# Half of one projection's columns multiplied inside the attention that runs before it

## The reference, cut to what matters

```python
proj = jnp.einsum('bsd,de->bse', rmsnorm(x, norm_w), w_in)
aq, ak, av, ag, bq, bk, bv, bg, iq, ik, iw = jnp.split(proj, split_at, axis=-1)
# group A: differential attention, 4 heads, two score maps each
p = softmax(q1 k1 * scale + bias) - lam * softmax(q2 k2 * scale + bias)
ao = rmsnorm(p v, subln_w) * (1 - lambda_init) * silu(ag)
# group B: 8 heads, each query sees only its 256 best keys by an indexer score
score = sum_h iw_h * relu(iq_h . ik);  sel = top_k(score, 256)
bo = softmax(q k[sel] * scale + bias) v[sel] * silu(bg)
y = x + concat(ao, bo) @ w_out;  return rmsnorm(y, final_norm_w)
```

## Time and profile before

| | us |
|---|---|
| median of 3 runs (lowest, highest) | 804.96 (803.58, 806.73) |
| the profiled execution: its time, its span | 805.53, 803.7 |
| first attention (PE's first score product to its last v product) | about 252.4 to 377 |
| projections of group B on PE | 377.5 to 551.8 |
| second half of the selection and the mask on DVE | 382.9 to 547.9 |
| second attention | 551.8 to about 700 |

### The profile page before, as it was taken

One profiled execution on the slowest core, in us unless ns is written; L12 is line 12 of the kernel. 1 busy time (PEld: TensorE's weight loads), 2 busy tenths in 40 slices (PEclk: granted clock), 3 DMA queues, 4 the chain that ended last, 5 costly groups with the idle time before them and its releaser, 6 DMA issues.

```text
span 803.7 us, 11774 instructions
## 1 busy us (share of the span) xinstructions
PE 759.5 (94%) x4161; PEld 634.3 (79%) x4161; DVE 630.1 (78%) x1347; ACT 305.3 (38%) x677; POOL 318.6 (40%) x383
## 2 busy tenths in 40 slices
PE   4899999999999888899999999999999999999996
PEld 3665888888887877788888888887888888888885
DVE  3738999999999988986999999996667676534343
ACT  5437222131315665677131220305545554422121
POOL 5220122124637775813255443647997600300000
PEclk9999999999999999999999999999999999999999
DMA  7142111111110101030211212110303100121231
GB/s 275 53 120 65 40 51 42 53 53 40 53 40 1 27 2 27 8 112 18 63 47 45 53 53 53 40 52 28 84 24 106 27 2 1 35 99 65 103 106 52
DMA packets 21489, 44.55 MB, mean 55 GB/s; under 512 B 3076, under 2 KB 5816, under 8 KB 21304
## 3 DMA queue, kind: packets, MB, share of 16 engines
q1 hardware_dynamic: 21432, 43.81, 18.5%
HBM read 35.40 MB, written 6.57 MB: 52 GB/s over the span
## 4 chain that ended last, share of the span: by engine, by line
PE 86%; DVE 7%; ACT 3%; issue 2%; DMA 1%; SPq 0%; POOL 0%; DVEq 0%; ACTq 0%
PE psum L990 43%; PE psum L1095 11%; PE psum L1153 11%; PE psum L1077 5%; PE psum L1052 4%; PE psum L1055 3%; PE psum L929 3%; PE psum L957 2%; DVE small L1331 2%; DVE probs L1385 1%; ACT probsT_B L804 1%; DVE small L1376 1%; DMA xs<-in_x 1%; PE psum L878 1%; PE psum L1063 1%
## 5 line engine op out<-in xcount | busy, mean ns | idle before, releaser
L511 POOL TENSOR_TENSOR w_lo<-w_raw,w_hi 128x512 fp32r<-128x512 f32 x64 | 83.1, 1300 | 244.4 <-ACT w_hi L660 244.0
L1312 DVE MATCH_REPLACE8 score<-top,score 128x384 f32<-128x384 f32 (+2 forms) x192 | 165.8, 876 | 0.0
L1307 DVE MAX8 top<-score 128x8 f32<-128x384 f32 (+2 forms) x192 | 155.5, 879 | 1.1
L660 ACT ACTIVATE w_hi<-w_raw 128x512 fp32r<-128x512 f32 x64 | 40.3, 630 | 240.4 <-PE psum L990 240.4
L990 PE MATMUL psum<-big_hi,w_hi 128*128 128x512 f32 x256 | 99.8, 390 | 0.3 <-POOL w_lo L511 0.3
L990 PE MATMUL psum<-big_hi,w_lo 128*128 128x512 f32 x256 | 99.6, 389 | 0.0
L990 PE MATMUL psum<-big_lo,w_hi 128*128 128x512 f32 x256 | 99.6, 389 | 0.0
L990 PE MATMUL psum<-w_hi,big_hi 128*128 128x512 f32 x256 | 99.6, 389 | 0.0
L990 PE MATMUL psum<-w_lo,big_hi 128*128 128x512 f32 x256 | 99.6, 389 | 0.0
L990 PE MATMUL psum<-w_hi,big_lo 128*128 128x512 f32 x256 | 99.6, 389 | 0.0
L793 ACT ACTIVATE probs<-psum,small 128x384 f32<-128x384 f32 (+7 forms) x112 | 83.0, 742 | 30.7 <-DVE small L1352 16.3
(11 more groups left out here) (156 smaller groups left out, 1505.4 us busy)
## 6 DMA issues: line engine op xcount, KB each, us to landing
w_raw<-in_w_in SPq DMA_DIRECT2D x64, 256.0 KB, 2.6
xs<-in_x SPq DMA_DIRECT2D x8, 512.0 KB, 6.5
k_high_twice<-k_high_twice SPq DMA_DIRECT2D x16, 256.0 KB, 3.7
xres<-in_x SPq DMA_DIRECT2D x8, 512.0 KB, 3.7
out_y<-y_out SPq DMA_DIRECT2D x16, 256.0 KB, 2.1
w_tail<-in_w_out SPq DMA_DIRECT2D x10, 256.0 KB, 2.6
bias_scratch<-bias_row SPq DMA_DIRECT2D x1, 2304.0 KB
bias<-bias_scratch SPq DMA_DIRECT2D x12, 128.0 KB, 3.1
```

The costliest lines, as they stand in the source:

```text
L511: pool.tensor_tensor(w_lo[:, r, 0:cols], w_raw[:, r, 0:cols], w_hi[:, r, 0:cols].bitcast(f32), ALU.subtract).then_inc(w_lo_made, 1)
L660: act.activation(w_hi[:, n % SW, 0:cols], w_raw[:, n % SW, 0:cols], ACT.Copy).then_inc(w_hi_made, 1)
L1307: ins = dve.max(top8[:, i - SEL0, :], sc)
L1312: ins = dve.match_replace(sc, top8[:, i - SEL0, :], sc, TAKEN)
```

## The change

The columns of group B's query projection (chunks 40 to 47) are cut differently: a chunk now is half of the 1024 rows (4 row blocks) of 128 columns. The first four chunks, `FILLS` = 40 to 43, which give column blocks 0 and 1 of the queries (four output banks), are multiplied inside the first attention: in iterations 1 to 32 PE does `fill`, three products of 512 columns, between the transposes of step s-1 and the map 1 scores. They gather in bank 4 (`FILL_BANK`), so the scores keep banks 0 to 3. Every 8th iteration ends a bank, and ACT moves it out (`move_fill`). After the attention PE does only the other half (`project_rest`), 96 products where there were 192, and goes on with the three other groups.

Chunks 40 to 43 get their own places: raw in slot 0 of `w_raw` and in a new `wf_raw`, the parts in `wf_hi` and `wf_lo`, which lie on what were a fourth `probs` buffer and `probs_x`. So `probs` has two buffers for map 0 and one for map 1.

```diff
+        Q_GROUP = B_GROUPS[0]
+        Q0 = Q_GROUP * DB
+        FILLS = range(Q0, Q0 + 4)
+        FILL_BANK = 4
...
-            if m == 0:
-                return probs[:, s % 3, :]
-            return probs[:, 3, :] if s % 2 == 0 else probs_x[:, 0, :]
+            return probs[:, s % 2 if m == 0 else 2, :]
-        S_BANKS, O_BANK, T_BANK = 5, 5, 6
+        S_BANKS, O_BANK, T_BANK = (4, 5), 5, 6
...   # sync: chunks 40 and 41 ahead of the key copies, 42 and 43 between them
-            for n in range(DB + SW, B_GROUPS[0] * DB):
+            for n in range(DB + SW, Q0 + 2):
                 load_chunk(n)
-            for b in range(BLOCKS):
-                copy_keys(0, b)
+            copy_keys(0, 0)
+            copy_keys(0, 1)
+            load_chunk(Q0 + 2)
+            load_chunk(Q0 + 3)
+            copy_keys(0, 2)
+            copy_keys(0, 3)
...   # gpsimd
             project_low(0)
+            low(Q0)
+            low(Q0 + 1)
+            wait_split(pool, Q0 + 1)
             split_part(0, 1, 0)
             split_part(0, 1, 1)
...
-                if s == STEPS - 4:
-                    low(B_GROUPS[0] * DB)
+                if s == 11:
+                    low(Q0 + 2)
+                elif s == 15:
+                    low(Q0 + 3)
+                elif s == STEPS - 4:
+                    low(Q0 + 4)
...   # scalar
+                        if g == A_GROUPS[-1] and d == DB - 1:
+                            high(Q0)
...
+                if s >= 1 and s % TILES == 0:
+                    move_fill(s // TILES - 1)
                 if s + 1 < STEPS:
                     exp(0, s + 1, 1)
-                if s == STEPS - 1:
-                    high(B_GROUPS[0] * DB)
+                if s == 0:
+                    high(Q0 + 1)
+                elif s == 13:
+                    high(Q0 + 2)
+                elif s == 17:
+                    high(Q0 + 3)
+                elif s == STEPS - 1:
+                    high(Q0 + 4)
...   # tensor
+            def fill(f, d):
+                c, half = column_block(f)
+                n = Q0 + 2 * c + d // 4
+                if d == 0 and f >= 1:
+                    pe.wait_ge(bank_moved, moved[Q_GROUP] + f)
+                if d % 4 == 0:
+                    wait_split(pe, n)
+                hi, lo = w_parts(n)
...
+                for k, (a, b) in enumerate(((hi, big_hi), (hi, big_lo), (lo, big_hi))):
+                    ins = pe.matmul(bank(FILL_BANK), a[:, ws], b[:, d, hs], start=(d == 0 and k == 0),
+                                    stop=(d == DB - 1 and k == 2))
...
                     for quad in qs[0:2]:
                         turn(ph, t, quad)
+                    if ph == 0 and s >= 1:
+                        fill((s - 1) // DB, (s - 1) % DB)
                     if s + 1 < STEPS:
                         scores(ph, s + 1, 1)
...
             attend(0)
-            for g in B_GROUPS:
+            project_rest()
+            for g in B_GROUPS[1:]:
                 project(g)
             attend(1)
```

More of the change, by code:

```diff
@@ L206, in build @@
         w_loaded = [sem(f"w_loaded{r}") for r in range(SW)]
+        wf_loaded = [sem(f"wf_loaded{r}") for r in range(2)]
         xres_loaded = [sem(f"xres_loaded{r}") for r in range(2)]
@@ L358, in wait_chunk_used @@
                 eng.wait_ge(bank_ready, before[g + 1])
-            else:
-                eng.wait_ge(chunk_used, (g - 1) * (DB - 1) + d + 1)
+            elif g == Q_GROUP and d % 2 == 1:
+                eng.wait_ge(bank_ready, before[g] + d + 1)
+            else:
+                fewer = 0 if g < Q_GROUP else d // 2 if g == Q_GROUP else 3
+                eng.wait_ge(chunk_used, (g - 1) * (DB - 1) + d + 1 - fewer)
         def wait_split(eng, n):
@@ L371, in w_staged, with w_parts, wait_loaded, same_slot @@
             r = n % SW
+            if n in FILLS:
+                return w_raw[:, 0, :] if n % 2 == 0 else wf_raw[:, :]
             return w_raw[:, r, :] if n < CHUNKS or r == 0 else w_tail[:, r - 1, :]
+        def w_parts(n):
+            if n in FILLS:
+                return wf_hi[:, n % 2, :], wf_lo[:, n % 2, :]
+            return w_hi[:, n % SW, :], w_lo[:, n % SW, :]
+        def wait_loaded(eng, n):
+            if n in FILLS:
+                eng.wait_ge(wf_loaded[n % 2], 16 * ((n - Q0) // 2 + 1))
+            else:
+                eng.wait_ge(w_loaded[n % SW], 16 * sum(k % SW == n % SW and k not in FILLS for k in range(n + 1)))
+        def same_slot(n):
+            if n in FILLS:
+                return n - 2 if n - 2 in FILLS else None
+            return max(k for k in range(n) if k % SW == n % SW and k not in FILLS)
         def units_before(ph, b):
@@ L451, in _ @@
                 load_bias(h)
-            for n in range(B_GROUPS[0] * DB + SW, CHUNKS):
+            for n in range(Q0 + 4 + SW, CHUNKS):
                 load_chunk(n)
@@ L704, in move @@
                 kind = GROUPS[g][2]
-                for t in range(8):
+                for t in range(4 if g == Q_GROUP else 0, 8):
                     act.wait_ge(bank_ready, before[g] + t + 1)
@@ L710, in move @@
                         is_q = g in (A_GROUPS[0], B_GROUPS[0])
-                        ins = act.activation((qT if is_q else kT)[:, c, cols], bank(t), ACT.Copy,
+                        ins = act.activation((qT if is_q else kT)[:, c, cols],
+                                             bank(t - 4 if g == Q_GROUP else t), ACT.Copy,
                                              scale=-QK_SCALE if is_q else 1.0)
@@ L720, in move, with move_fill @@
                     ins.then_inc(bank_moved, 1)
+            def move_fill(f):
+                act.wait_ge(bank_ready, before[Q_GROUP] + f + 1)
+                c, half = column_block(f)
+                act.activation(qT[:, c, half * HALF:(half + 1) * HALF], bank(FILL_BANK), ACT.Copy,
+                               scale=-QK_SCALE).then_inc(bank_moved, 1)
             def project(groups, last):
```

86 lines of the change are left out of this document (63 added, 23 removed).

## The result

The changed kernel takes 816.9 us (median of 4, 816.05 to 817.46), the kernel before, run beside it, 804.6: ratio 1.0149, 95% interval [1.0136, 1.0161]. The profiled execution grew from a span of 803.7 to 815.7 us, that is by 12.0; the forecast had 9.3 more, 814.3 for the median.

A forecast was written before the change was run, and what follows sets the result against it. DVE's selection and mask, not PE, were taken to end B's projections, and a PE, DVE and ACT chain to bound the first attention; 0 + 3.1 + 4.9 + 1.3 = 9.3 us gave 814.8, as median 814.3, range 807.5 to 822.

The forecast's parts named there:

- Step 1: Projections of B: 96 products fewer, 21.8 us of PE, gain 0, because DVE's mask and then ACT are late next.
- Step 2: First attention: fills of 0.68 us PE work in 32 iterations mostly fit under pauses; 3.1 us show, bounds 1 to 11.
- Step 3: First attention, block 1: POOL's low part of chunk 41 waits for ACT, delaying the keys; PE waits 4.9 us, bounds 3.5, 7.
- Step 4: Start of the second attention: after 22 us of idling PE restarts at half rate, costing 1.3 us, bounds 0 to 2.4.
- Rival A: First attention: the fills cost far more, 11 us in place of 3.1, giving 822 us; chance 0.18.
- 4 to 7: Sign at block 1's first scores: one PE wait of 4 to 7 us with a key copy or POOL as releaser.
- POOL slowed by DVE: Block 1's key wait: upper bound of 7 us if POOL's operations are slowed by DVE work they now run beside.
- no wait would stand at block 3: First attention: PE's wait for keys appears only at block 1, none at blocks 2 and 3.
- blocks 1 to 3 growing by more than 1.5 us each: First attention: growth of these blocks beyond 1.5 us each was named as a sign that the prediction is wrong.
- B: Whole kernel: no difference to speak of; POOL's detour costs nothing and the clock does not matter, 808 us; chance 0.10.
- C: Projections of B: PE is the bound after all, so the second attention starts earlier, 792 us; chance 0.04.
- D: Block 2 or 3: a fill waits for chunk 42 or 43 and stops PE some 5 us, 819 us; chance 0.03.

The follow-up runs named there:

- quiet run: Changed kernel with POOL's low parts of chunk 41 and the fourth early chunk later, and POOL waiting for DVE's six masks before second-attention block 1 splits: 806.6 us, 1.0020.
- shortened kernel before: The kernel before with two of the 16 selection rounds after the first attention left out: 804.4 us, 0.9998 of the kernel before.
- split first: Changed kernel with POOL making the low part of chunk 41 after block 1's two query parts, not ahead of them: 810.6 us, 1.0077 of the kernel before.
- the tail is spread: Quiet run with mixB rows reversed, two longest tiles' masks before the last selection round, gate moves waiting only for masks of what they overwrite: 802.0 us, 0.9965.
- best version: The kernel in which the tail is spread, with 16 fills in place of 32 in the first attention, at steps with room: 798.6 us, 0.9918.
- shortened changed kernel: The changed kernel with the same two selection rounds left out as in the shortened kernel before: 795.6 us, 0.9888 of the kernel before.

## Why the prediction was right, and where it was off

The direction, the range and the main mechanism were right: PE's work left a stage whose end PE does not set, and entered one where every microsecond counts. The sum was 2.7 us short. Two terms were too small, by 1.8 and 1.4 us, and one was 0.9 too large, so part of the nearness is luck.

| step of the prediction | forecast, us | measured, us |
|---|---|---|
| 1, products leave the projections | 0 | 0 |
| 2, fills in the attention | 3.1 | 4.9 |
| 3, POOL's detour | 4.9 | 6.3 |
| 4, clock behind the long pause | 1.3 | about 0.4 |
| attention begins earlier (252.02), scatter | - | -0.3 |
| masks beside POOL | - | 0.65 |
| sum | 9.3 | 12.0 |

*Step 1* held in each of its signs: selection of the same length, ACT waiting 34 us for the mask (about 30 forecast), the exponential 6.7 us behind it, PE idle for 22.3 us. The two shortened kernels show the cause and not only the fit. What it left out: the masks themselves became 0.65 us longer (7.01 against 6.36), for POOL is busy beside them for 6.54 us, with block 1's splits, which PE's early end allows, and not for 5.85, with those of block 0. Even the 6.36 of before were mostly POOL's doing: the masks take 2.70 us in the quiet run, and 3.46 in the shortened kernel before, where POOL is busy for 0.90 beside them and PE works throughout.

*Step 2* was sized by single gaps of one block. Where it stands alone, in "split first" against before, it is 1.19 us in block 0, 0.47 in block 1, 0.90 in block 2 and 2.34 in block 3; forecast were 0.6 (the rest was to hide in the wait of point 3), 0.8, 0.8 and 0.9. It went right for the long tiles and for tile 0, and was too high for tile 2 (0.3 in place of 0.54, by step 14: 2.55 us against 2.24). It went wrong in block 3, as if only its last two iterations lacked cover:

```profile
346.33:377.23 30.90, 28.65 (x204) 25.46 (x202) 24.07 (x53) 21.95 (x67) 4.68 (x9) 1.00 0.19 59
348.56:381.80 33.24, 33.20 (x231) 30.39 (x231) 24.16 (x53) 22.93 (x69) 4.14 (x8) 1.00 0.19 52
```

The first row is block 3 before, the second in "split first". POOL has no splits left there (4.68 us busy, against 22.71 in block 2), DVE runs faster beside it (the `combine` of 1024 keys takes 1.28 us, in blocks 1 and 2 2.38; DVE's sum is 24.07 us against 28.36), and PE is already the busiest engine. With the fills it is busy for 33.20 of 33.24 us: in block 3 PE sets the pace, and there is no gap for a fill. The term took the gaps of another block for those of this one. Rival A (fills for 11 us) did not come true; 4.9 lies nearer to the forecast.

*Step 3* had the mechanism and the shift (283.2 forecast, 282.94 in the trace). Mis-sized was what came with it. Block 1 starts at 287.66, 5.5 us later than before and not 4.9, though the wait in PE's row is only 3.55 us, under the 4 to 7 that the prediction named as its sign: PE was through with its own work at 284.1 and not at 282.2, 0.9 us of it by the fills and 1.1 by DVE in step 2, held up by POOL's late splits. And the sum did not have the half clock behind the wait (1.55 us). So the detour costs 3.55 + 1.1 + 1.6 = 6.3. The prediction put "POOL slowed by DVE" into its bounds; it was DVE that was slowed. It also said that no wait would stand at block 3; one of 0.94 us did.

The prediction named blocks 1 to 3 growing by more than 1.5 us each as a sign of being wrong. They grew by 2.07, 0.91 and 2.35: two of the three went over it, for the two reasons just told.

*Step 4* had the fall of the clock but not its price. The rows of the changed kernel:

```profile
545.00:562.00 17.00, 0.00 (x0) 0.00 (x0) 14.32 (x21) 2.49 (x4) 15.54 (x19) 0.50 0.00 0
562.00:564.00 2.00, 0.60 (x2) 0.50 (x2) 0.00 (x0) 2.00 (x5) 1.92 (x3) 0.50 0.87 207
564.00:566.00 2.00, 2.00 (x7) 1.06 (x6) 1.05 (x5) 1.98 (x3) 1.92 (x3) 0.50 0.63 186
566.00:568.00 2.00, 2.00 (x9) 1.70 (x9) 1.41 (x5) 1.68 (x5) 1.92 (x3) 0.50 0.43 131
568.00:572.00 4.00, 4.00 (x34) 3.70 (x33) 3.44 (x13) 2.58 (x5) 3.83 (x5) 0.99 0.40 134
```

1.2 GHz from the first product at 563.40 to 568, 4.6 us; here the clock has fallen within the pause. Most of it fell on scores that ran beside ACT's moves and table load, so the lag behind the kernel before grew only from 11.54 us at the exponential to 11.93 at the scores of 568.44. I had priced eight slow microseconds on PE without asking how many of them something waits for. The same clock that was overpriced here was missing in step 3, where everything waits for PE. It is dearer again once the tail is spread: in the best version the eight transposes behind the first exponential take 1.85 us in place of 1.28, and the scores behind them start 2.71 us after that exponential (549.59 - 546.88), before 1.92 (556.51 - 554.59).

*The rivals.* B (no difference) and C (faster) fell with the shortened kernels and the 22.3 us pause; D did not occur, as PE never waited for a raw chunk.

Left open: why the first row of the attention scatters by up to 2 us between runs (250.99 to 253.04), and why the clock fell within one pause of under four microseconds and not within another (see the last section).

## What to carry to other kernels

Work taken from an engine pays only where that engine's end sets the next stage; read the end of the stage (which row releases whom) and test it by shortening the other engine's work, in both kernels. Before work is moved into a stage, lay a step clock over it (one row per step) and fill the steps that have room, not all. An operation put into the order of a side engine costs what stands behind it there; where it waits for a third engine, put the urgent ones first. And what a side engine does earlier or later meets other work: look which operations of its neighbour become longer.

## What the runs showed of the hardware

- TensorE's granted clock after a pause. After 3.55 us of pause in the changed kernel the products started at 2.4 GHz, the clock fell half a microsecond later and stayed at 1.2 GHz for 3.4 us. In the pause of 3.82 us of the best version it fell within the pause, at about 542.8, and work went on at 1.2 GHz from 544.15 to about 549.7, 5.5 us. After 22.3 us of pause the low rate lasted 4.6 us of work. After the pauses of 0.94 and 1.47 us at block 3, and of 0.93 us in the shortened changed kernel, it stayed at 2.4 GHz. The longest pause was not followed by the longest slow stretch.
- Six DVE mask operations took 2.70 us with POOL idle and 6.36 to 7.01 with POOL splitting beside them; the selection's MAX8 and MATCH_REPLACE8 were not slowed (158.6 us with and without). A one-column DVE operation took 1.32 us in place of 0.22 when it met a POOL operation of 1.28 us. That both end together speaks for waiting, not for shared bandwidth. By this the trace agrees with the Trainium skill, page "SBUF — State Buffer", section "Who interferes with whom": DVE and GpSimd share one pair of ports, and it is "an exclusive lock", so the second one is blocked until the first has finished. Whether the masks meet the page's conditions for using that pair is shown here by nothing but this slowing. The advice of the Trainium skill on the same page, section "Summary: rules for kernel authors", to look which of the two is off the critical path, holds with a price here: one wait on POOL, ahead of splits that nothing needed yet, gave 5.0 us.
